# Band attention scores over 64 rows of the array, and a fourth gate among the band steps

## What is computed

```python
def swa_attention(q, k, v, rel_bias, sinks):          # 8 chunks of 64 queries, 16 heads of 64, 2 key groups
    q = q.reshape(B, n_chunks, CHUNK, SWA_KV_HEADS, SWA_GROUP, SWA_HEAD_DIM)
    kb, vb = band(k), band(v)                         # each chunk sees its own 64 keys and the 64 before
    logits = jnp.einsum('bcqhgd,bckhd->bchgqk', q, kb).astype(jnp.float32) * (SWA_HEAD_DIM ** -0.5)
    logits = logits + rel_bias.reshape(SWA_KV_HEADS, SWA_GROUP, CHUNK, W * CHUNK)
    m = jnp.maximum(jnp.max(logits, axis=-1, keepdims=True), sink)
    p = jnp.exp(logits - m)
    p = (p / (jnp.sum(p, axis=-1, keepdims=True) + jnp.exp(sink - m))).astype(vb.dtype)
    o = jnp.einsum('bchgqk,bckhd->bcqhgd', p, vb)
...
    g_mla, g_swa = jnp.split(jax.nn.sigmoid(h @ w_gate[l]), N_BRANCHES, axis=-1)
    x = x + (g_mla * y_mla + g_swa * y_swa) @ w_out[l]
```

## Time and profile before

| | |
|---|---|
| median of 3 runs | 1123.16 us (1122.78 to 1123.64) |
| the profiled execution | 1122.71 us, span of its instructions 1120.9 us |
| TensorE busy | 1110.6 us (99%) |
| weight loads busy | 909.7 us (81%) |
| VectorE, ScalarE, GpSimd busy | 567.1, 418.9, 149.1 us |
| from HBM | 93 GB/s over the span, 512 KB units land in 3.3 to 3.4 us |

### The profile page before, as it was taken

One profiled execution on the slowest core, in us unless ns is written; L12 is line 12 of the kernel. 1 busy time (PEld: TensorE's weight loads), 2 busy tenths in 40 slices (PEclk: granted clock), 3 DMA queues, 4 the chain that ended last, 5 costly groups with the idle time before them and its releaser, 6 DMA issues.

```text
span 1120.9 us, 14768 instructions
## 1 busy us (share of the span) xinstructions
PE 1110.6 (99%) x5198; PEld 909.7 (81%) x5198; DVE 567.1 (51%) x852; ACT 418.9 (37%) x719; POOL 149.1 (13%) x119
## 2 busy tenths in 40 slices
...
PEclk9999999999999999999999999999999999999999
...
GB/s 261 86 103 123 100 94 94 94 102 103 95 70 125 105 94 59 14 142 57 118 69 65 71 99 94 95 94 94 94 97 106 98 94 94 94 94 103 88 71 76
DMA packets 35262, 107.21 MB, mean 96 GB/s; under 512 B 4224, under 2 KB 7968, under 8 KB 35216
## 3 DMA queue, kind: packets, MB, share of 16 engines
...
...
## 4 chain that ended last, share of the span: by engine, by line
PE 97%; DVE 1%; ACT 1%; issue 0%; POOL 0%; DVEq 0%; POOLq 0%; ACTq 0%
PE bank L1352 29%; PE bank L1354 29%; PE bank L1353 29%; PE bank L1494 2%; PE bank L1524 1%; PE bank L1689 1%; PE bank L1691 1%; PE bank L1690 1%; PE bank L1549 1%; PE bank L1484 1%; PE bank L1534 1%; PE bank L1468 1%; PE bank L1462 0%; PE bank L1461 0%; PE bank L1460 0%
## 5 line engine op out<-in xcount | busy, mean ns | idle before, releaser
L617 ACT ACTIVATE w_hi<-staged 128x1024 fp32r<-128x1024 f32 x182 | 193.0, 1061 | 544.1 <-PE bank L1354 544.0
L1352 PE MATMUL bank<-xg_hi,w_hi 128*128 128x512 f32 x1000 | 394.9, 395 | 0.0
L1354 PE MATMUL bank<-xg_hi,w_lo 128*128 128x512 f32 x1000 | 389.5, 389 | 0.0
L1353 PE MATMUL bank<-xg_lo,w_hi 128*128 128x512 f32 x1000 | 389.3, 389 | 0.0
L922 DVE TENSOR_TENSOR w_lo<-staged,w_hi 128x1024 fp32r<-128x1024 f32 x182 | 225.5, 1239 | 108.5 <-ACT w_hi L617 108.4
L1352 PEld LDWEIGHTS bank<-xg_hi,w_hi 128*128 128x128 f32 x1000 | 187.7, 188 | 44.2 <-issue 6.1
L1354 PEld LDWEIGHTS bank<-xg_hi,w_lo 128*128 128x128 f32 x1000 | 187.7, 188 | 39.6
L1353 PEld LDWEIGHTS bank<-xg_lo,w_hi 128*128 128x128 f32 x1000 | 187.9, 188 | 38.3 <-issue 0.7
L511 POOL TENSOR_TENSOR h_lo<-hid,h_hi 128x512 f32 x44 | 70.6, 1604 | 591.2 <-ACT h_hi L640 534.9
L1352 PE MATMUL bank<-h_hi,w_hi 128*128 128x512 f32 x304 | 118.4, 389 | 0.2 <-POOL h_lo L511 0.2
L1353 PE MATMUL bank<-h_lo,w_hi 128*128 128x512 f32 x304 | 118.3, 389 | 0.0
...
## 6 DMA issues: line engine op xcount, KB each, us to landing
...
```

Source lines behind the costliest of these rows:

```text
L617: nc.scalar.activation(w_hi[:, u % SPLIT, :], staged[:, u % STAGED, :], ACT.Copy).then_inc(hi_done, 1)
L1352: nc.tensor.matmul(o, wh, hi, start=start, stop=False)
L1353: nc.tensor.matmul(o, wh, lo, start=False, stop=False)
L1354: return nc.tensor.matmul(o, wl, hi, start=False, stop=stop)
```

## The change

The eight matmuls of a chunk are made together, in `band_scores(c)`, on even steps. Each takes 64 rows of the array, those of its own key group, and 128 columns of keys, and the two groups write different banks (4 and 5). `ks` loses its zeros: one plane, one write by VectorE, 64 cleared columns. A step now belongs to a key group and not to half the heads, so the bias is read with a stride, the sinks are laid out anew, and the band values are two matmuls of 512 columns on every second step. The visit of a chunk stands behind the transposes of the even step and waits for both exponentials of the chunk before. Scores of chunk 0, which were made ahead of the last query product (group half 0) and behind the first latent half, are both made behind the first latent half. The plan of fillers is rearranged: four gates instead of three lie among the band steps, gate 0 ends at step 5 instead of 8, latent tile 1 is used up at step 0 instead of 1, latent tile 4 at step 7 instead of 6, and ahead of step 0 stand three halves instead of two. The gates get a seventeenth place in memory, since the latent tiles are still in use when the fourth is made.

```diff
--- before.py
+++ after.py
@@ -62,8 +62,8 @@
-EARLY_GATES = 3
-GATE_SLOTS = (2, 5, 4, 0) + tuple(range(6, 16)) + (1, 3)
+EARLY_GATES = 4
+GATE_SLOTS = (2, 5, 4, 16) + tuple(range(6, 16)) + (1, 3)
 W_STEPS, M_STEPS = NC * 2, MH * TT
 STEPS = W_STEPS + M_STEPS
@@ -74,22 +74,22 @@
 def fillers():
-    plan = [halves("latent", 0),
-            [("latent", 1, 0)],
-            [("latent", 1, 1), ("latent", 2, 0)],
+    plan = [halves("latent", 0) + [("latent", 1, 0)],
+            [("latent", 1, 1)],
+            [("latent", 2, 0)],
             [("latent", 2, 1), ("sum", 0, "kv")],
             [("kpe", 0, 0), ("root", 0, "kv"), ("rest", 2, "q"), ("latent", 3, 0)],
             [("newton", 0, "kv"), ("latent", 3, 1)],
-            [("scale", 0, "kv"), ("latent", 4, 0)],
-            [("round", 0, "kv"), ("rest", 3, "q"), ("latent", 4, 1)],
-            [("rest", 0, "kv"), ("gate", 0, 0)],
-            [("rest", 4, "q"), ("gate", 0, 1), ("kpe", 0, 1), ("sum", 0, "q"), ("uk", 0, 0)],
-            [("uk", 1, 0), ("uk", 2, 0), ("root", 0, "q")],
-            [("split", 1, "gate"), ("uk", 3, 0), ("uq", 0, 0)],
-            [("uq", 1, 0), ("gate", 1, 0)],
-            [("gate", 1, 1)],
+            [("scale", 0, "kv")] + halves("gate", 0),
+            [("round", 0, "kv"), ("rest", 3, "q"), ("latent", 4, 0)],
+            [("rest", 0, "kv"), ("latent", 4, 1)],
+            [("rest", 4, "q"), ("kpe", 0, 1), ("uk", 0, 0), ("uk", 1, 0)],
+            [("sum", 0, "q"), ("uk", 2, 0), ("gate", 1, 0)],
+            [("split", 0, "uq"), ("uk", 3, 0), ("gate", 1, 1)],
+            [("root", 0, "q"), ("split", 2, "gate"), ("uq", 0, 0), ("uq", 1, 0)],
             [("gate", 2, 0)],
-            [("gate", 2, 1), ("uv", 0, 0)],
+            [("gate", 2, 1), ("gate", 3, 0)],
+            [("gate", 3, 1), ("uv", 0, 0)],
             [("uv", 1, 0), ("uv", 2, 0)],
             [("uv", 3, 0)]]
     todo = [("uq", t, 0) for t in range(2, 6)]
...
@@ -235,7 +235,7 @@
         probs_t = sb("probs_t", [P, 2, S], f32, mix)
         rot = sb("rot", [P, S], f32, mix)
         mask_sb = sb("mask_sb", [P, P])
-        ks = sb("ks", [P, SKV, CHUNK + S], f32, mix)
+        ks = sb("ks", [P, CHUNK + S], f32, mix)
         turn_sb = sb("turn_sb", [P, P])
         vs_t = probs[:, :, :].rearrange("p a b -> p (a b)")[:, 0:CHUNK + S]
         gsum = probs
...
@@ -455,7 +454,7 @@
             sources = {"latent": w_in, "gate": w_gate, "uq": w_uq, "uk": (w_uk,), "uv": (w_uv,)}
             for (kind, t), w in UNIT_AT.items():
-                if w == UNIT_AT["gate", 1]:
+                if w == UNIT_AT["gate", 2]:
                     sp.wait_ge(lat_ready, 2)
                     sp.dma_start(lat[:, 0, :], rope_2).then_inc(rope_in, 16)
                 elif w == UNIT_AT["uq", 1]:
@@ -530,7 +529,7 @@
             ffn_program(0, NORM_MIX, send_bias_rows)
             pool.wait_ge(grp_ready, MIX_G)
-            pool.memset(ks[:, :, :], 0.0).then_inc(ks_clear, 1)
+            pool.memset(ks[:, 0:CHUNK], 0.0).then_inc(ks_clear, 1)
             for n in (NORM_KV, NORM_Q):
                 clear_acc(n)
@@ -828,8 +827,6 @@
             for w in range(U_FILL):
-                if w == U_FILL - 1:
-                    exponentials(0)
                 split_hi(u + w + SPLIT)
                 if w == 1:
                     x_norm_root(NORM_MIX)
@@ -839,6 +836,7 @@
                         nc.scalar.activation(vband[:, 4 * half:4 * half + 4, :].rearrange("p a b -> p (a b)"),
                                              bank[S_BANK + half][:, :], ACT.Copy).then_inc(vband_ready, 1)
+            exponentials(0)
             exponentials(1)
             for piece in PLAN[0]:
                 filler(*piece)
@@ -1108,16 +1106,14 @@
                 if n >= 2:
                     dve.wait_ge(exp_done, n - 1)
                 if n < W_STEPS:
-                    c, half = n // 2, n % 2
+                    c, kv = n // 2, n % 2
                     tiles = b[:, :].rearrange("p (t k) -> p t k", t=4)
-                    done(nc.vector.tensor_tensor(b[:, :], b[:, :],
-                                                 bias[:, 2 * half:2 * half + 2].rearrange("p a b c -> p (a b c)"),
-                                                 ALU.add))
+                    done(nc.vector.tensor_tensor(tiles, tiles, bias[:, :, kv, :], ALU.add))
                     if c == 0:
                         done(nc.vector.memset(tiles[:, :, 0:CHUNK], NEG))
                     done(nc.vector.tensor_reduce(smax[:, n % 2, :], tiles, AX.X, ALU.max, negate=True))
-                    done(nc.vector.tensor_tensor(nmax[:, n % 2, :], smax[:, n % 2, :], sink_neg[:, half, :], ALU.min))
-                    nc.vector.tensor_tensor(sinkd[:, n % 2, :], sink[:, half, :], nmax[:, n % 2, :], ALU.add)\
+                    done(nc.vector.tensor_tensor(nmax[:, n % 2, :], smax[:, n % 2, :], sink_neg[:, kv, :], ALU.min))
+                    nc.vector.tensor_tensor(sinkd[:, n % 2, :], sink[:, kv, :], nmax[:, n % 2, :], ALU.add)\
                         .then_inc(max_ready, 1)
                 else:
                     i = m_step(n)[1]
@@ -1243,18 +1239,11 @@
                     split_lo(u + 1 + SPLIT)
                     make_rms(NORM_MIX)
                     b = bank[(g + U_KS) % 4]
-                    dve.wait_ge(ks_clear, 1)
-                    for h in range(SKV):
-                        rows = slice(h * SD, (h + 1) * SD)
-                        e = nc.vector.tensor_tensor(ks[rows, h, CHUNK:CHUNK + S], b[rows, :], rms[rows, :], ALU.mult)
-                    e.then_inc(grp_read, 1)
+                    nc.vector.tensor_tensor(ks[:, CHUNK:CHUNK + S], b[:, :], rms[:, :], ALU.mult).then_inc(grp_read, 1)
                     dve.wait_ge(grp_ready, g + U_VS + 1)
                     nc.vector.memset(vs_t[:, 0:CHUNK], 0.0)
                     nc.vector.tensor_tensor(vs_t[:, CHUNK:CHUNK + S], bank[(g + U_VS) % 4][:, :], rms[:, :], ALU.mult)\
                         .then_inc(grp_read, 1)
-                if w == U_FILL - 1:
-                    dve.wait_ge(bias_in, 16 * SG)
-                    scores(0)
                 if w >= U_QS:
                     dve.wait_ge(grp_ready, g + w + 1)
                     t = w - U_QS
@@ -1265,8 +1254,10 @@
                                                    op0=ALU.mult, op1=ALU.mult).then_inc(grp_read, 1)
                     split_lo(u + w + SPLIT)
+            dve.wait_ge(bias_in, 16 * SG)
+            scores(0)
+            scores(1)
             normalise(0)
-            scores(1)
             for piece in PLAN[0]:
                 filler(*piece)
             for n in range(STEPS):
@@ -1470,29 +1461,33 @@
             u, g = MIX_U, MIX_G
+            def band_scores(c):
+
+                if c == 0:
+                    pe.wait_ge(vband_ready, 2)
+                    pe.wait_ge(ks_clear, 1)
+                    pe.wait_ge(grp_read, g + G_QS + SG)
+                else:
+                    pe.wait_ge(exp_done, 2 * c)
+                for pair in range(SG // 2):
+                    for kv in range(SKV):
+                        rows = slice(kv * SD, (kv + 1) * SD)
+                        last = nc.tensor.matmul(bank[S_BANK + kv][:, pair * BAND:(pair + 1) * BAND],
+                                                qs[rows, pair, c, :, :].rearrange("p a b -> p (a b)"),
+                                                ks[rows, c * CHUNK:c * CHUNK + BAND], start=True, stop=True)
+                        if pair == SG // 2 - 1:
+                            last.then_inc(s_ready, 1)
+
             def scores(n):
                 b = bank[S_BANK + n % 2]
-                if n < 2:
-                    pe.wait_ge(vband_ready, 2)
-                    pe.wait_ge(grp_read, g + G_QS + 4 * (n + 1))
-                else:
-                    pe.wait_ge(exp_done, n - 1)
-                if n < W_STEPS:
-                    c, half = n // 2, n % 2
-                    for j in range(2):
-                        pair = 2 * half + j
-                        last = nc.tensor.matmul(b[:, j * 2 * BAND:(j + 1) * 2 * BAND],
-                                                qs[:, pair, c, :, :].rearrange("p a b -> p (a b)"),
-                                                ks[:, :, c * CHUNK:c * CHUNK + BAND], start=True, stop=True)
-                    last.then_inc(s_ready, 1)
-                else:
-                    h, i = m_step(n)
-                    if i == 0:
-                        pe.wait_ge(grp_read, g + GROUP_AT["uq", Q_NOPE[h // 2]] + 1)
-                        pe.wait_ge(q_spread[h // 2], 16 * 4)
-                        pe.wait_ge(kpe_spread, 16)
-                    nc.tensor.matmul(b[:, 0:query_keys(i)], qm[:, h, norm_rows(i)], km[:, h, 0:query_keys(i)],
-                                     start=True, stop=True).then_inc(s_ready, 1)
+                pe.wait_ge(exp_done, n - 1)
+                h, i = m_step(n)
+                if i == 0:
```

(38 more changed lines are left out.)

11 lines of the change are left out of this document (5 added, 6 removed).

## The result

The changed kernel takes 1124.58 us (median of 20, 1123.41 to 1125.23), the kernel before 1122.99 (median of 20, 1122.34 to 1123.64): ratio 1.0014, 95% interval 1.0008 to 1.0021. The forecast was 1121.6 us, a little faster; it came out a little slower. The profiled execution took 1124.83 us, its span is 1123.0, both 2.1 more than before.

The account below looks back on a forecast made before the run. The prediction took TensorE, busy 99% of the span, to bound the kernel. From the profiled 1122.71 us, -4.95 (TensorE) + 3.7 (waits) + 0.2 (latent steps) = -1.05 gave 1121.6 us, range 1117.5 to 1126.5.

Parts of the forecast that it names:

- walk for what is late next: Following every engine's program order through the band steps for new TensorE waits: +3.7 us net.
- switches: Band visits: going in and out of the split array costs TensorE 1.75 us together (0.7 to 2.8).
- latent steps: Latent steps after the fourth gate moves out: two more lack a filler, costing 0.2 us (0.2 to 0.4).
- TensorE's sum: Band visits: overlapping row halves save 6.7 us, mode changes cost 1.75 us, together -4.95 us.
- Case C: Band scores: row halves don't overlap because one loader feeds both; 1128.7 us, 1126 to 1130, chance 0.15.
- First wait: After band visit 0: step 0 waits because VectorE has both steps' scores ahead of the denominators; 0.5 to 0.6 us.
- Second: After latent tile 1 ends, step 0: GpSimd adds its squares before scaling step 2; 1.0 us.
- Third: Step 2's scores wait for exponentials 3, counted from the end of latent tile 1; 0.35 us.
- Fourth wait: Band visit 5: gate 0 ending at step 5, with ScalarE's table load and Tanh, delays exponentials 9; 1.9 us.
- Fifth: After visit 5: the query sum waits until VectorE has read the turned key; 0.5 us.
- From step 9 on I find no wait: Band steps from step 9: slots hold 18 or 24 matmuls, so no TensorE wait was expected.
- Case D: Row halves overlap but waits double to 8 us, VectorE's small operations stretching beside GpSimd; 1123.8 to 1127 us, chance 0.13.

Follow-up runs that it names:

- e8: The changed kernel with a band visit's eight products ordered group after group, all of key group 0 and then all of group 1, instead of alternating; 1127.84 us.
- e3: The changed kernel with GpSimd scaling the probabilities of step 2 first and adding the squares of latent tile 1 afterwards; 1123.21 us.
- e4: The changed kernel with ScalarE taking gate 0's Tanh and its table load five steps later, at the place of gate 1's; 1124.36 us.
- e9: The changed kernel with e3's GpSimd order, the turned key one step earlier and the fourth key tile ahead of the second gate; 1124.15 us.
- e2: The changed kernel with the earlier kernel's step plan: three early gates, its filler order, and the rope load behind gate 1; 1126.52 us.
- e14: The changed kernel with e3's GpSimd order, turned key at step 7, second gate at steps 8 and 9 ahead of the key tiles; 1119.89 us.
- e15: The kernel of e14 with band scores multiplied over all 128 rows, both groups' scores summed in each bank; 1125.22 us.

## Why the prediction was wrong

The step that failed is the walk for what is late next: it gave +3.7 us of waits and they measure +4.9, with the reason of one wrong, one over twice its size and three overlooked. Smaller misses are the switches, the latent steps and the clock.

- **TensorE's sum** (predicted -6.7 and +1.75). Right in mechanism, near in size. The saving is 8 x (1.72 - 0.87) = 6.8 us. The switches are 6 x 0.22 + 0.42 + 0.48 = 2.2 us, inside the bounds and 0.45 over the value taken: a third mode between two others cost 0.22, not half of 0.35. Case C, row halves that don't overlap, is excluded; e8 shows what it would have looked like.
- **The sums**: two of the walk are off as written. The third's terms give 4.88 us, not 4.95, the fourth's chain 10.8, not 10.9; neither moves the result by more than 0.2 us.
- **First wait**: 0.46 us (0.55 predicted), right. **Second**: 1.40 (1.0), right place, and e3 confirms GpSimd's addition as its end, but taking it away gives back only part, because the third stands right behind it. **Third**: 0.19 (0.35), hidden by the second.
- **Fourth wait** (1.9 us, from the table load at step 5). It measured 0.85 and the reason fell: e4 moved the load and nothing changed. The step that failed is the walk from the end of gate 0 through Tanh to exponentials 8. I had ScalarE's pieces in one unbroken row, when it waits twice in it for others. The chain that is last starts at the band visit itself: it takes 9.59 us to the next visit in the changed kernel and in e9 alike, and e9 hides it with the key's product.
- **Fifth**: 1.0 us and 0.46 behind it (0.5), right place, two to three times the size: among others an operation of VectorE stretched beside GpSimd, 0.77 us for 0.16. How much of the wait that is, no run shows.
- **"From step 9 on I find no wait"** was false. The second gate needs the query sum's bank read, and VectorE reads it behind scores 11 (0.74), held up in the trace by a denominator operation of 1.21 us for 0.16, beside GpSimd once more; the query products wait for their split (0.48). I had checked products against time there, not which bank or buffer each piece takes.
- The waits sum to 0.46 + 1.40 + 0.19 + 0.85 + 1.0 + 0.46 + 0.74 + 0.48 = 5.6 us, less 0.66 that goes: +4.9, against +3.7. This is the largest of the misses and by itself turns the forecast -1.05 to +0.15. The latent steps cost +0.7, not +0.2; e2 with its three gates has the old length. Some score and transpose matmuls start later than others with equal work, as the second of these two shows (0.43 and 0.54 to the transpose behind), but no run shows that this is the whole 0.7.
```profile
552.18 0.59 PE L1489 MATMUL bank<-km,qm 128*128 128x256 f32 x2
552.62 0.27 PE L1516 MATMUL bank<-idn,probs 128*128 128x128 f32 x1
...
553.84 0.70 PE L1489 MATMUL bank<-km,qm 128*128 128x256 f32 x2
554.38 0.27 PE L1516 MATMUL bank<-idn,probs 128*128 128x128 f32 x1
```
- With the measured terms, -6.8 + 2.2 + 4.9 + 0.7 = +1.0 us; the mixing stage of the first trace is 1.19 longer, 0.2 of it not assigned.
- **The clock** "should stay at its upper level": it doesn't, in about half the executions (15 of 31 at 0.996 or less), and that is about 1.1 us in each of these. Of the 3.0 us between 1121.6 and the median of 1124.58 the clock makes 0.7, the terms above 2.05 (-1.05 to +1.0), and 0.3 is that the forecast starts from the profiled 1122.71 and not from the median of 1122.99. I had taken a slice row of the kernel before, in which TensorE never stands still, as if it held for one in which it does. Case D's range holds the measured time with a partly right reason: VectorE's stretched operations are there, but the waits are 5.6 us, not 8, and the clock and the switches make up for it. That it fits is luck.

That the waits, not the size of the gain, decided is shown by e14 with e15: same row halves, waits of about 2 us in place of 5.6, time 1119.9, and 5.3 us lost when the halves are taken away.
